# FOX attention: a pair of heads scored in one segment, forget sums by products on all rows, the meta queries in one batch

## The chip, the cores and the metric

One core of a Trainium2 chip. The metric is the device time of one launch in microseconds (us), the median of several runs. Five engines work beside each other: TensorE (PE; its weight loads are PEld), VectorE (DVE), ScalarE (ACT), GpSimd (POOL) and SyncE (SP, which issues the weight DMAs). Data lie in SBUF, products arrive in PSUM, which has 8 banks of 512 float32 columns on 128 partitions.

## What is computed

A decoder over 272 tokens: 16 meta tokens and 256 real ones, 1024 features. Four layers (FOX, GLA, GDN, FOX mixers, each with a SwiGLU), then two further layers of another kind. The change concerns the FOX mixer, which stands in layers 0 and 3. After an RMS norm and the projection to q, k, v, gate and forget logits (16 heads of 64):

```python
log_f = jax.nn.log_sigmoid((f + b_f).astype(jnp.float32))
c = jnp.cumsum(log_f, axis=1).transpose(0, 2, 1)
s = jnp.einsum('bqhd,bkhd->bhqk', q, k)          # q, k normalised per head
s = jnp.where(kpos[None, :] <= qpos[:, None], s + cq[..., :, None] - ck[..., None, :], -jnp.inf)
o = jnp.einsum('bhqk,bkhd->bqhd', jax.nn.softmax(s, axis=-1), v)
out = (o * jax.nn.sigmoid(gate)) @ w_out
```

The query's own sum cq is the same along a row and drops out of the softmax; the kernel adds only the key's. Real queries come in two blocks of 128: block A sees 144 keys (the meta tokens and itself), block B all 272. The 16 meta queries see the 16 meta keys. In layer 3 the outputs of meta tokens are not needed any more, so there the meta queries are left out.

## The kernel before, in words

All projections run with features on partitions and tokens as the moving columns. float32 accuracy comes from splitting weights and activations into a high and a low part (`ring_hi`, `ring_lo` and `y_r`, `y_lo_r`, type float32r): a tile of 128 outputs is 8 x 3 products of 128x128 by up to 272 columns (line 773, called from `blocks`). Weights stream through four ring slots; ScalarE makes the high half (line 1549, `split`), VectorE the low half (line 2113), in the FOX stage each at every second tile.

The FOX projection has 32 tiles in the order q, k, v of each of the 8 head pairs (two heads of 64 features fill 128 partitions), then 8 gate tiles (`FOX_TILES`). The attention of a pair is placed between tiles: TensorE calls `middle(t)` halfway through tile t and `after(t)` behind it. Each engine runs its own program in a fixed order; semaphores connect them. For pair c:

- after tile 3c+4, part A, after 3c+5 part B, after 3c+6 part M (the meta queries, FOX 0 only). For each part: `scores`, one tile later `turn` (transposes of the probabilities), one tile later again `values`.
- `scores` (955): for both heads a float32 product of 64 rows (two instructions each), the two heads beside each other in the array, then a product of a 2-row ones matrix with the head's forget sums (high and low part, rows 0 and 1 of `f_c_r`), one for each head.
- VectorE `largest` (2258) adds the mask and takes the least value of each row in one instruction; ScalarE `exponent` (1690) takes the exponential and the row sum; VectorE `inverse` (2271); GpSimd multiplies (2932); TensorE `turn` (995) transposes into bank 4 or 5; ScalarE `take_turned` (1677) copies; TensorE `values` (1019) accumulates into bank 6, again both heads beside each other on column halves, in key blocks of 128, 128 and 16; ScalarE copies the output.
- the q and k tiles of a pair need a statistic each (`statistic`, 979: sum of squares per head, in bank 7), after the next tile. ScalarE takes logarithm and exponential (`rstd_of`, 1660), VectorE refines it by Newton steps and scales (`head_norm`, 2218; lines 2129, 2135, 2136, 2225). The k statistic may not overwrite bank 7 before the first Newton step of q has read it (`stat_taken`).
- the v tile is transposed in `middle` (988) by three transposes of 128, 128 and 16 tokens.
- the forget sums are made once by VectorE (`forget_sums`, 2228) on 16 partitions, brought by two GpSimd DMAs to two partitions (2923, 2924) and rounded there by eight copies (2927).

VectorE's order in a tile slot t: `inverse` of the slot before, `head_norm` of tile t-2, the evacuation of tile t, `largest`, then the weight split. ScalarE's: `rstd_of`, output copy, `take_turned`, `take_tokens`, the square for the statistic, the weight split, `exponent`. After the last part, gates are applied (2279), and the result is split again for the output projection `fox_out`, by GpSimd for the pairs 0 to 4 and by ScalarE and VectorE for 5 to 7.

## Time and profile before

| | |
|---|---|
| median of three runs | 2334.38 us (2331.07 to 2335.42) |
| span of the profiled execution, first to last instruction | 2328.9 us |
| the times of the runs themselves, each with what lies around the span | 2331.07, 2334.38, 2335.42 us |
| TensorE busy (matmul side) | 2246.5 us, 96% |
| VectorE busy | 1538.0 us, 66% |
| ScalarE busy | 1186.7 us, 51% |
| GpSimd busy | 603.7 us, 26% |
| mean granted clock of TensorE | 0.992 |

How to read it: the engines' times overlap, so they don't add up. A product occupies the array for less than its record lasts, since the next starts before it ends; the distance between two starts is what it costs in a full stream. float32 products are recorded as two instructions, float32r products and transposes as one. Idle time of an engine is put down to what released it. FOX 0 lies from about 10 to 181 us, FOX 1 from 1205 to 1357 us.

### The profile page before, as it was taken

The page shows a single profiled execution, that of the slowest core. Times are in us where ns is not written, and L with a number is a line of the kernel's source. Part 1 is how long each engine was busy: PE and PEld are TensorE (multiplying, and loading weights), DVE is VectorE, ACT ScalarE, POOL GpSimd, SP SyncE. Part 2 cuts the span into 40 slices and gives each one's busy share as a digit, 9 for nine tenths or more (in the row PEclk, how much of TensorE's full clock was granted, in tenths as well). Part 3 has the DMA queues.
Part 4 walks back from the last instruction along what each step waited for, and adds up shares of the span by engine and source line. Part 5 has one row for each costly group of instructions (what it writes and reads, how often), then busy time and mean ns, then how long its engine had stood idle before and what let it go on. Part 6 is the DMA issues. An engine that isn't in the chain of part 4 may idle for free.

```text
span 2328.9 us, 48307 instructions
## 1 busy us (share of the span) xinstructions
PE 2246.5 (96%) x19152; PEld 2129.8 (91%) x19152; DVE 1538.0 (66%) x2490; ACT 1186.7 (51%) x1849; POOL 603.7 (26%) x741
## 2 busy tenths in 40 slices
PE   8999999899999999899999999998999999999998
PEld 7889999899999789899998899997789998798998
DVE  6656554656555776655556566657768976767994
ACT  5555544445544643455346554544556654556653
POOL 1114211003221030122111141217135535134540
PEclk9999999999999999999999999999999999999999
DMA  5224546324546321255552345564354555343554
GB/s 211 92 92 164 179 154 192 125 87 161 172 162 192 115 74 56 73 169 175 160 174 102 109 163 181 165 202 149 109 191 164 182 168 177 107 145 127 187 171 131
DMA packets 53007, 344.03 MB, mean 148 GB/s; under 512 B 5920, under 2 KB 7136, under 8 KB 20448
## 3 DMA queue, kind: packets, MB, share of 16 engines
q1 hardware_dynamic: 52128, 336.26, 43.7%
q0 software_dynamic: 704, 5.31, 0.6%
q8 instruction: 126, 2.06, 0.4%
q14 instruction: 49, 0.40, 0.1%
HBM read 340.43 MB, written 1.05 MB: 147 GB/s over the span
## 4 chain that ended last, share of the span: by engine, by line
PE 80%; DVE 9%; ACT 5%; issue 3%; DMA 1%; POOL 1%; DVEq 0%; ACTq 0%; SPq 0%; POOLq 0%
PE ps L773 78%; ACT ring_hi L1549 3%; DVE ring_lo L2113 2%; ACT arena L1549 1%; PE ps L1001 1%; DMA ring<-in 0%; DVE newt L2135 0%; DMA ring<-out 0%; DVE newt L2129 0%; PE ps L1435 0%; ACT rstd L1549 0%; DVE hrs L2136 0%; DVE arena L2796 0%; DMA ring<-gdn_in 0%; ACT L1549 0%
## 5 line engine op out<-in xcount | busy, mean ns | idle before, releaser
L773 PE MATMUL ps<-arena_r,ring_hi 128*128 128x272 f32 (+1 forms) x6688 | 1578.7, 285 | 9.9 <-DVE arena_r L2628 5.5
L773 PEld LDWEIGHTS ps<-arena_r,ring_hi 128*128 128x128 f32 x6688 | 1155.1, 189 | 18.1 <-issue 11.2
L773 PE MATMUL ps<-y_r,ring_hi 128*128 128x272 f32 (+1 forms) x3424 | 1003.9, 293 | 15.4 <-DVE arena L2436 5.4
L2113 DVE TENSOR_TENSOR ring_lo<-ring,ring_hi 128x2048 fp32r<-128x2048 f32 (+3 forms) x373 | 739.8, 1984 | 360.4 <-ACT ring_hi L1549 360.0
L773 PE MATMUL ps<-y_r,ring_lo 128*128 128x272 f32 (+1 forms) x3424 | 973.2, 284 | 0.0
L773 PEld LDWEIGHTS ps<-y_r,ring_hi 128*128 128x128 f32 x3424 | 646.0, 189 | 39.4 <-issue 13.7
L1549 ACT ACTIVATE ring_hi<-ring 128x2048 fp32r<-128x2048 f32 (+3 forms) x373 | 611.6, 1643 | 89.9 <-DMA ring<-dn 47.8
L773 PEld LDWEIGHTS ps<-y_r,ring_lo 128*128 128x128 f32 x3424 | 648.2, 189 | 0.0
L773 PE MATMUL ps<-arena_r,ring_lo 128*128 128x256 f32 (+1 forms) x1632 | 463.8, 284 | 0.0
L773 PEld LDWEIGHTS ps<-arena_r,ring_lo 128*128 128x128 f32 x1632 | 307.5, 188 | 0.0
L1549 ACT ACTIVATE arena<-arena 128x272 f32<-128x272 f32 (+7 forms) x197 | 91.0, 464 | 381.3 <-DVE arena L2700 257.2
L3016 POOL CAST arena_r<-arena 128x272 fp32r<-128x272 f32 (+1 forms) x132 | 134.7, 1021 | 536.0 <-DVE arena L2702 419.5
L773 PE MATMUL ps<-arena 64*64 64x64 f32 (+18 forms) x2792 | 204.4, 264 | 12.3 <-ACT arena L1549 11.2
L773 PEld LDWEIGHTS ps<-arena 64*64 64x64 f32 (+9 forms) x2792 | 144.2, 142 | 55.5 <-issue 25.9
L3024 POOL TENSOR_SCALAR arena<-x,par 128x256 f32<-128x256 f32 (+1 forms) x91 | 88.4, 971 | 305.6 <-ACT y_r L1549 304.7
L1549 ACT ACTIVATE sq<-x 128x256 f32<-128x256 f32 (+1 forms) x120 | 50.3, 419 | 187.3 <-DVE x L2164 186.5
L1549 ACT ACTIVATE arena<-ps 128x256 f32<-128x256 f32 (+7 forms) x291 | 91.7, 363 | 75.0 <-PE ps L773 32.2
L3017 POOL TENSOR_TENSOR arena_r<-arena,arena_r 128x272 fp32r<-128x272 f32 (+1 forms) x132 | 102.4, 776 | 10.6
L2741 DVE SCALAR_TENSOR_TENSOR arena<-arena,par 128x256 f32<-128x256 f32 x176 | 99.5, 623 | 0.0
L1549 ACT ACTIVATE arena<-arena,par 128x256 f32<-128x256 f32 (+1 forms) x112 | 62.0, 582 | 67.1 <-DVE arena L2677 47.7
L1549 ACT ACTIVATE arena<-arena,neg_max 128x144 f32<-128x144 f32 (+3 forms) x104 | 47.7, 459 | 83.4 <-DVE neg_max L2267 50.3
L2932 POOL TENSOR_SCALAR arena<-arena,row_inv 128x144 f32<-128x144 f32 (+2 forms) x72 | 33.4, 469 | 212.4 <-DVE row_inv L2277 212.2
(244 smaller groups left out, 1689.7 us busy)
## 6 DMA issues: line engine op xcount, KB each, us to landing
ring<-gu SPq DMA_DIRECT2D x88, 1024.0 KB, 5.1
ring<-dn SPq DMA_DIRECT2D x64, 704.0 KB, 4.1
ring<-up SPq DMA_DIRECT2D x44, 1024.0 KB, 5.2
ring<-fox_in SPq DMA_DIRECT2D x31, 1024.0 KB, 5.2
ring<-sdn SPq DMA_DIRECT2D x32, 704.0 KB, 4.1
ring<-gdn_in SPq DMA_DIRECT2D x16, 1024.0 KB, 5.2
ring<-in SPq DMA_DIRECT2D x16, 1024.0 KB, 5.2
ring<-gla_in SPq DMA_DIRECT2D x12, 1024.0 KB, 5.1
```

What stands on the lines that cost most here:

```text
L773: return nc.tensor.matmul(dst, w, mv, start=start, stop=stop)
L1001: last = nc.tensor.transpose(ps[0:w, 4 + u % 2, q * P:q * P + un["qn"]], un["p"][0:un["qn"], a:a + w], ident[0:un["qn"], 0:un["qn"]])
L1549: return nc.scalar.activation(dst, src, f, **kw)
L2113: V.tensor_tensor(ring_lo[:, slot, cols], ring[:, slot, cols], ring_hi[:, slot, cols].bitcast(F32), ALU.subtract).then_inc(lo_ready, 2 if ...
L2741: V.scalar_tensor_tensor(out=u_cc[:, q, :], in0=u_gp[:, q, 1 + tap:1 + tap + SEQ], scalar=par[:, bass.ds(i * 24 + (w0 + 12 * b + 3 * q + 1 ...
L2932: G.tensor_scalar(p, p, row_inv[0:un["qn"], u % 4:u % 4 + 1], 1.0, ALU.mult, ALU.mult).then_inc(p_ready, 1)
L3016: step(G.tensor_copy(hi_r[:, c, :], lo[:, c, :]))
L3017: G.tensor_tensor(lo_r[:, c, :], lo[:, c, :], hi_r[:, c, :].bitcast(F32), ALU.subtract).then_inc(h_split, 1)
L3024: step(G.tensor_scalar(lo[:, c, :], src[:, c, :], pcol(gain, c), 1.0, ALU.mult, ALU.mult))
```

## The change

- The four parts A0, A1, B0, B1 of a pair become one unit: after tile 3c+4 TensorE computes, for both heads, 144 and then 272 columns of scores side by side in one bank a head (416 columns, banks 2 and 3), and VectorE and ScalarE handle four blocks in a row (`least`, `exponents`, `inverses`).
- The forget sums stay where VectorE makes them: `f_sums_r` holds the high parts on partitions 0 to 15, the low parts on 32 to 47, zero elsewhere, with the 144 keys and the 272 keys side by side. A 128x128 weight of zeros with ones in the head's two rows (`f_pick_r`, 16 of them, made by GpSimd) picks a head's: one product of 128 rows and 416 columns for a head. DMAs and copies go.
- The 16 meta keys of the two heads are put block-diagonal: `f_px` has the probabilities of head 0 in columns 0 to 15, those of head 1 in 16 to 31, zero elsewhere, and `f_vsrc` the meta tokens' values likewise, each head's features only in its own columns. All blocks turned are 128x128 (eight a pair, in `middle` of tile 3c+6, four to a bank, copied by ScalarE as 512 columns). `values` comes after tile 3c+7, ahead of the next pair's scores: one product for the meta keys of both heads, then the other key blocks on column halves, the key block that both query blocks share with 256 columns at once.
- The meta queries of all eight pairs (FOX 0) are one batch at the last pair: narrow scores into bank 5, one product for their sums, three small VectorE steps, one exponential, three more, two transposes, a widened block-diagonal copy, one product of 512 columns, two copies out. The gate and the split of their outputs for pairs 0 to 6 are three VectorE instructions after the last tile (`meta_gated`), and the first product of `fox_out0` waits for them.
- Tables: three small constants more (80 columns of the constants' load).
- ScalarE's sigmoid for the gates may start two tiles earlier.

The diff, cut to its core; the bodies that it replaces stand above:

```diff
-FOX_PARTS = {"A0": (META, META + P, 0), "A1": (META, META + P, 1), "B0": (META + P, T, 0), "B1": (META + P, T, 1), "M": (0, META, 0)}
+FOX_KEYS = [META + P, T]
+FOX_SPAN = [slice(0, META + P), slice(META + P, META + P + T)]
+FOX_QUERIES = [slice(META, META + P), slice(META + P, T)]
+FOX_LAST = 3 * (KC - 1) + 4
+META_SUMS, META_SCORED, META_LEAST, META_EXP, META_P, META_TURNED, META_SPREAD, META_SUMMED, META_TAKEN, META_SPLIT = 1, 2, 3, 4, 5, 6, 8, 9, 10, 11
...
+def fox_scored(t):
+    return (t - 4) // 3 if t % 3 == 1 and 4 <= t <= FOX_LAST else None
+def fox_turned(t):
+def fox_weighed(t):
+    return (t - 7) // 3 if t % 3 == 1 and 7 <= t <= FOX_LAST + 3 else None
...
             def fox(name, nb, tpb, kc):
                 j = int(name[-1])
-                units = fox_units(j)
-
                 first_tile = n.tile
...
+                later = META + P
+                def scores(c):
+                    pe.wait_ge(head_ready, n.head + 2 * c + 2)
+                    if c == 0:
+                        pe.wait_ge(pick_ready, j + 1)
+                        pe.wait_ge(c_ready, j + 1)
                     else:
...
+                        pe.wait_ge(max_ready, n.unit + 4 * c)
+                    for part, (keys, span, queries) in enumerate(zip(FOX_KEYS, FOX_SPAN, FOX_QUERIES)):
+                        for m in range(2):
+                            r = slice(m * FD, (m + 1) * FD)
+                            mm(ps[:, 2 + m, span], f_q[r, c, queries], f_k[r, c, 0:keys], part == 0, False)
+                    if j == 0 and c == KC - 1:
+                        meta_scores()
+                    for m in range(2):
+                        mm(ps[:, 2 + m, 0:later + T], f_pick_r[:, 2 * c + m, :], f_sums_r[:, :], False, True).then_inc(s_ready, 2)
+                def meta_scores():
+                    pe.wait_ge(ptok_ready, n.unit + 4 * (KC - 1))
+                    pe.wait_ge(meta_chain, META_SUMS)
+                    for c in range(KC):
+                        for m in range(2):
+                            r = slice(m * FD, (m + 1) * FD)
+                            mm(ps[m * 32:m * 32 + 32, 5, c * META:(c + 1) * META], f_q[r, c, 0:32], f_k[r, c, 0:META], c == 0, False)
+                    mm(ps[0:64, 5, 0:P], f_parity_r[:, :], f_msum_r.rearrange("p c k -> p (c k)"), False, True).then_inc(meta_chain, 1)
...
+                def turn(c):
+                    pe.wait_ge(p_ready, n.unit + 4 * c + 4)
+                    pe.wait_ge(metas_scaled, 2 * (KC * j + c + 1))
+                    if c:
+                        pe.wait_ge(ptok_ready, n.unit + 4 * c)
                     for m in range(2):
...
+                        blocks_ = [f_pa[:, m, META:later], f_pb[:, m, META:later], f_pb[:, m, later:T], f_px[:, m, :]]
+                        if m and c == KC - 1 and j == 0:
+                            pe.wait_ge(meta_chain, META_LEAST)
+                        for q, a in enumerate(blocks_):
+                            last = nc.tensor.transpose(ps[:, 4 + m, q * P:(q + 1) * P], a, ident)
+                        last.then_inc(pt_ready, 2)
+                def meta_turn():
+                    pe.wait_ge(meta_chain, META_P)
+                    pe.wait_ge(max_ready, n.unit + 4 * KC)
+                    nc.tensor.transpose(ps[:, 2, 0:64], f_pm[0:64, :, :].rearrange("p c k -> p (c k)"), ident[0:64, 0:64])
+                    nc.tensor.transpose(ps[:, 3, 0:P], f_vmeta[:, :], ident).then_inc(meta_chain, 1)
+                def values(c):
+                    pe.wait_ge(ptok_ready, n.unit + 4 * c + 4)
+                    pe.wait_ge(vtok_ready, n.vtok + c + 1)
+                    if c:
+                        pe.wait_ge(o_taken, j * KC + c)
+                    mm(ps[:, 6, META:T], f_vtok[:, c % 2, 2, :], f_pt[:, :, 3 * P:4 * P], True, False)
+                    for m in range(2):
+                        r = slice(m * FD, (m + 1) * FD)
+                        mm(ps[r, 6, META:T], f_vtok[:, c % 2, 0, r], f_pt[:, m, 0:2 * P], False, False)
+                    for m in range(2):
+                        r = slice(m * FD, (m + 1) * FD)
+                        last = mm(ps[r, 6, later:T], f_vtok[:, c % 2, 1, r], f_pt[:, m, 2 * P:3 * P], False, True)
+                    last.then_inc(pv_ready, 4)
+                def meta_outputs():
+                    pe.wait_ge(meta_chain, META_SPREAD)
+                    mm(ps[:, 3, :], f_mv[:, :], f_mspread.rearrange("p c q -> p (c q)")).then_inc(meta_chain, 1)
                 def middle(t):
+                    if fox_turned(t) is not None:
+                        turn(fox_turned(t))
+                        if j == 0 and fox_turned(t) == KC - 1:
+                            meta_turn()
                 def after(t):
                     if t == 1 and j == 0:
                         pe.wait_ge(consts_loaded, 16)
                     if t == 0:
                         narrow(ps[0:FH, 6, 0:T], j * P, FH, 1 + 3 * j, FH).then_inc(narrow_ready, 1)
...
+                        meta_outputs()
+                    if fox_weighed(t) is not None:
+                        values(fox_weighed(t))
+                    if fox_scored(t) is not None:
+                        scores(fox_scored(t))
                     if t:
                         part, c = FOX_TILES[t - 1]
                         if part in "qk":
                             statistic(part, c)
-                    for u in in_slot(units, t - 1):
...
                 def ready(k):
+                    if meta and k == 0:
+                        pe.wait_ge(meta_chain, META_SPLIT)
                     if k >= late:
                         pe.wait_ge(late_split, n.late + k - late + 1)
                     else:
...
+                def take_turned(c):
+                    if c:
+                        act.wait_ge(pv_ready, n.unit + 4 * c)
+                    for m in range(2):
+                        act.wait_ge(pt_ready, n.unit + 4 * c + 2 * m + 2)
+                        fn(f_pt[:, m, :], ps[:, 4 + m, :], ACT.Copy).then_inc(ptok_ready, 2)
+                def exponents(c):
+                    for u in range(4):
+                        act.wait_ge(max_ready, n.unit + 4 * c + u + 1)
+                        fn(fox_p(u), fox_p(u), ACT.Exp, scale=-1.0, bias=neg_max[:, u:u + 1], accum_out=row_sum[:, u:u + 1]).then_inc(exp_ready, 1)
...
+                    keys = slice(META + P, META + P + T)
+                    step(V.tensor_copy(f_sums_r[0:FH, keys], f_rows[0:FH, 4, :]))
+                    step(V.tensor_tensor(f_sums_r[32:32 + FH, keys], f_rows[0:FH, 4, :], f_sums_r[0:FH, keys].bitcast(F32), ALU.subtract))
+                    V.tensor_copy(f_sums_r[0:48, 0:META + P], f_sums_r[0:48, META + P:2 * (META + P)].bitcast(F32)).then_inc(c_ready, 1)
                     n.logit += 1
...
+                def least(c):
+                    if c:
+                        v.wait_ge(pt_ready, n.unit + 4 * c)
+                    elif j == 0:
                         v.wait_ge(consts_loaded, 16)
...
+                def inverses(c):
+                    if c:
+                        v.wait_ge(metas_scaled, 2 * (KC * j + c))
+                    for part in range(2):
+                        v.wait_ge(exp_ready, n.unit + 4 * c + 2 * part + 2)
+                        V.reciprocal(row_inv[:, 2 * part:2 * part + 2], row_sum[:, 2 * part:2 * part + 2]).then_inc(inv_ready, 1)
...
+                def meta_gated():
+                    v.wait_ge(meta_chain, META_TAKEN)
+                    v.wait_ge(gate_ready, n.gate + KC - 1)
+                    o, hi = f_o[:, 0:KC - 1, 0:META], f_hi_r[:, 0:KC - 1, 0:META]
+                    step(V.tensor_tensor(o, o, f_gate[:, 0:KC - 1, 0:META], ALU.mult))
+                    step(V.tensor_copy(hi, o))
+                    V.tensor_tensor(f_o_r[:, 0:KC - 1, 0:META], o, hi.bitcast(F32), ALU.subtract).then_inc(meta_chain, 1)
...
+                G.memset(f_sums_r[:, :].bitcast(F32), 0.0).then_inc(sums_clear, 1)
+                step(G.memset(f_vsrc[:, :], 0.0))
+                step(G.memset(f_px[:, :, :], 0.0))
+                if j == 0:
+                    pool.wait_ge(consts_loaded, 16)
+                    G.tensor_copy(f_parity_r[:, :], const("fox_parity"))
+                G.tensor_tensor(f_pick_r[:, :, :], over(ident[:, 0:FH], P), over(ident[:, 32:32 + FH], P), ALU.add).then_inc(pick_ready, 1)
+                if j == 0:
+                    pool.wait_ge(c_ready, 1)
+                    pool.wait_ge(sums_clear, 1)
+                    G.tensor_tensor(f_msum_r[:, :, :], each(f_sums_r[:, META + P:META + P + META].bitcast(F32), KC), over(const("fox_pair"), META), ALU.mult).then_inc(meta_chain, 1)
+                sides = halves.rearrange("p (s x) -> p s x", s=2)[:, :, 0]
+                def place(c):
+                    pool.wait_ge(evacuated, BANKS + tiles + 3 * c + 3)
+                    if c:
+                        pool.wait_ge(vt_ready, KC * j + c)
+                    metas = f_v[:, c % 2, 0:META]
+                    if j == 0:
+                        G.tensor_copy(f_vmeta[:, c * META:(c + 1) * META], metas)
+                    G.tensor_tensor(f_vsrc[:, 0:2 * META].rearrange("p (s k) -> p s k", s=2), each(metas, 2), over(sides, META), ALU.mult).then_inc(metas_placed, 1)
+                place(0)
                 for c in range(KC):
...
+                    for part, p in enumerate((f_pa, f_pb)):
+                        pool.wait_ge(inv_ready, n.inv + 2 * c + part + 1)
+                        for m in range(2):
+                            u = 2 * part + m
+                            G.tensor_scalar(p[:, m, META:], p[:, m, META:], row_inv[:, u:u + 1], 1.0, ALU.mult, ALU.mult).then_inc(p_ready, 1)
+                        G.tensor_tensor(f_px[:, part, 0:2 * META].rearrange("p (s k) -> p s k", s=2), p[:, :, 0:META],
+                                        over(row_inv[:, 2 * part:2 * part + 2], META), ALU.mult).then_inc(metas_scaled, 1)
+                    if c + 1 < KC:
+                        place(c + 1)
+                n.inv += 2 * KC
```

## Rows read from the trace of the kernel before

**Rows 1.** The page: busy shares and the clock granted to TensorE in 40 slices.

```profile
PE 2246.5 (96%) x19152; PEld 2129.8 (91%) x19152; DVE 1538.0 (66%) x2490; ACT 1186.7 (51%) x1849; POOL 603.7 (26%) x741
...
PEclk9999999999999999999999999999999999999999
```

**Rows 2.** Busy time by window; start:end and length, each engine's us (instructions), PEclk, DMA.

```profile
20.74:23.74 3.00, 3.00 (x26) 3.00 (x25) 2.16 (x6) 1.39 (x2) 0.00 (x0) 1.00 0.21 86
30.03:33.66 3.63, 3.63 (x18) 3.52 (x17) 3.56 (x6) 1.33 (x3) 1.90 (x3) 0.53 0.04 10
38.22:180.98 142.76, 142.07 (x1138) 118.75 (x1138) 86.40 (x225) 81.43 (x234) 24.87 (x52) 1.00 0.30 100
82.36:99.18 16.82, 16.82 (x135) 13.82 (x134) 11.17 (x28) 10.67 (x30) 2.20 (x5) 1.00 0.18 64
1223.03:1356.80 133.77, 132.31 (x1034) 111.52 (x1034) 84.47 (x201) 78.14 (x214) 26.07 (x46) 1.00 0.32 107
1281.75:1297.33 15.58, 15.58 (x122) 13.08 (x121) 8.50 (x24) 8.47 (x26) 2.02 (x4) 1.00 0.42 136
```

**Rows 3.** TensorE's waits from 1205 to 1357 us: total us, times, longest.

```profile
PE ps L773 <- DVE newt L2129: 1.2, 2, 1.0
```

**Rows 4.** TensorE's timeline of a pair: start, us from start to last end, instructions.

```profile
70.97 0.52 PE L773 MATMUL ps<-arena 64*128 64x144 f32 x4
71.41 0.44 PE L773 MATMUL ps<-arena_r 2*128 2x144 f32 x2
71.78 0.73 PE L773 MATMUL ps<-sq,con 128*128 128x272 f32 x2
...
72.59 1.02 PE L773 MATMUL ps<-arena 128*64 128x128 f32 x12
73.54 0.39 PE L773 MATMUL ps<-y_r,ring_hi 128*128 128x272 f32 x1
...
76.74 0.73 PE L773 MATMUL ps<-arena 64*128 64x272 f32 x4
77.40 0.52 PE L773 MATMUL ps<-arena_r 2*128 2x272 f32 x2
77.84 0.73 PE L773 MATMUL ps<-sq,con 128*128 128x272 f32 x2
78.41 0.60 PE L1001 MATMUL ps<-con,arena 128*128 128x128 f32 x4
78.94 0.29 PE L773 MATMUL ps<-arena 16*64 16x16 f32 x4
```

**Rows 5.** VectorE's timeline of a pair: minima, weight split, Newton step.

```profile
88.70 0.31 DVE L2267 CUSTOM_DVE_ANT_0 arena<-ps,con 128x144 f32<-128x144 f32 x1 [0.37 <-PE ps L773]
...
94.76 0.44 DVE L2267 CUSTOM_DVE_ANT_0 arena<-ps,con 128x272 f32<-128x272 f32 x1 [0.66 <-PE ps L773]
...
95.13 0.44 DVE L2267 CUSTOM_DVE_ANT_0 arena<-ps,con 128x272 f32<-128x272 f32 x1
...
95.49 2.29 DVE L2113 TENSOR_TENSOR ring_lo<-ring,ring_hi 128x2048 fp32r<-128x2048 f32 x1
...
97.83 0.42 DVE L2129 SCALAR_TENSOR_TENSOR newt<-ps,hrs 128x272 f32<-128x272 f32 x1
```

**Rows 6.** ScalarE's timeline of a pair: exponentials, then the statistic's logarithm.

```profile
89.05 0.41 ACT L1549 ACTIVATE arena<-arena,neg_max 128x144 f32<-128x144 f32 x1 [0.26 <-DVE neg_max L2267]
...
95.25 0.52 ACT L1549 ACTIVATE arena<-arena,neg_max 128x272 f32<-128x272 f32 x1 [2.54 <-DVE neg_max L2267]
...
95.77 0.51 ACT L1549 ACTIVATE arena<-arena,neg_max 128x272 f32<-128x272 f32 x1
...
96.28 0.47 ACT L1549 ACTIVATE hrs<-ps,con 128x272 f32<-128x272 f32 x1
```

**Rows 7.** GpSimd's timeline: two probabilities times the inverses of their sums.

```profile
97.95 1.15 POOL L2932 TENSOR_SCALAR arena<-arena,row_inv 128x272 f32<-128x272 f32 x2 [7.31 <-DVE row_inv L2277]
```

**Rows 8.** TensorE's timeline at the entry of FOX 0, its wait in brackets.

```profile
29.70 0.82 PE L773 MATMUL ps<-sq,con 128*128 128x272 f32 x2 [2.33 <-DVE newt L2129]
```

281 lines of the change are left out of this document (105 added, 176 removed).

## The prediction

> **What bounds the kernel now.** I read the page's shares first, then two stretches as windows, TensorE's waits, and one pair of heads as a timeline on each engine. TensorE's matmul side is busy 96% of the span and its granted clock is full almost everywhere [rows 1]: the end is set by how much TensorE has to issue. The change touches the two FOX stages. From the first pair's scores to the last projection tile they take 142.76 us (FOX 0) and 133.77 us (FOX 1), with VectorE busy 60 to 63% of that [rows 2]. TensorE waits little there: 1.2 us on VectorE from 1205 to 1357 us, most of it at the stage's entry [rows 3]. So what is taken off TensorE's own stream shortens the kernel, until another engine is late.
>
> Durations overlap in the pipeline, so I price by the distance between starts [rows 4]. A projection tile of 24 products is 3.00 us when nothing interrupts it (first window of [rows 2]). A steady pair (three tiles, 9.0 us) takes 16.82 us in FOX 0 and 15.58 us in FOX 1 [rows 2]; 7.8 us of the former are attention.
>
> **Prices from [rows 4].** Scores of both heads: 0.45 us at 144 keys (70.97 to 71.41), 0.66 us at 272. The 128 further columns in 2 instructions a head cost 0.21 to 0.22 us, so one column in one instruction is 0.84 ns (two passes), both heads beside each other. Then 144 columns need 0.24 us and 272 need 0.46; the other 0.20 us is what changing the shape in which the array is used (64x128 after 128x128, and away again) costs. The forget products on 2 rows: 0.37 and 0.44 us for two single-pass products that should stream 0.12 and 0.23, again 0.2 of change. A statistic is 0.57 us (77.84 to 78.41) with one such change, 0.46 without. Four transposes plus the change behind them are 0.53 us: 0.11 each, whether 16 or 128 columns wide. The 12 value instructions are 0.95 us (72.59 to 73.54).
>
> **The change part by part, one pair.**
> - Scores: one segment of 144 and 272 keys with one change of shape: 0.24 + 0.46 + 0.20 = 0.90 us (before 0.45 + 0.66, and 0.33 for the pair's meta cells).
> - Forget sums: two products on 128 rows over 416 columns, single pass: 416 x 0.42 ns = 0.18 each, and 0.10 for going back to the full array: 0.47 us (before 0.37 + 0.44). No row of before has 416 columns: below it is bounded by 0.35 (no change cost), above by 0.35 + 0.20 + 0.10.
> - Statistics: both now follow full-array work, 2 x 0.46 = 0.92 us (before some 0.66 + 0.57).
> - Values: a full-array product of 256 columns (0.43), then column halves 256 (0.43) and 128 columns (0.22), changes 0.25: 1.33 us. Streamed columns hardly fall (640 against 656); three groups become one. Between 1.2 and 1.5.
> - Transposes: 8 in one go 0.87 us and 3 for the values 0.33; none of them changes the shape. The 16-column ones already cost as much as whole ones.
>
> Sum 4.82 us, so a pair is 9.0 + 4.8 = 13.8 us of TensorE in FOX 0, 13.65 in FOX 1, where a query tile streams 256 columns (3.00 - 24 x 16 x 0.42 ns = 2.84 us).
>
> The stretches: FOX 0 = 27 tiles 81.1 + 8 x 1.37 scores and sums 11.0 + values 10.8 + 14 statistics 6.4 + 7 x 0.33 + 8 x 0.87 = 118.6, and the batch for the meta queries: 32 narrow score instructions (some 0.03 each with changes: 1.2), the parity product and two transposes 0.3, one product over 512 columns 0.86: 2.3. That is 120.9 us. FOX 1 = 13 tiles at 3.00, 14 at 2.84, and 37.5: 116.3 us.
>
> **What becomes late.** This is the part that can undo it. TensorE's next fixed points after a pair's scores are the key statistic of the next pair (it shares a bank with the query statistic, so it waits until VectorE's first Newton step has read that), and the pair's turn, half a tile later. Let X be the end of tile 3c+4. Values now go ahead of scores: the first head's scores stand at X + 1.33 + 0.90 + 0.29 + 0.2 latency = X + 2.7 (before X + 1). VectorE's queue is then: four minima (0.3, 0.3, 0.37, 0.36 [rows 5]) to X + 4.0; in every other pair the weight split, 2.29 us, to X + 6.2; the reciprocals, which wait for all exponentials; the Newton step, 0.42. ScalarE: four exponentials 0.41, 0.41, 0.52, 0.51 from X + 3.05, to X + 4.9, then the statistic's logarithm and exponential 0.93, to X + 5.85 [rows 6]. TensorE is back after 3.16 us of this group and a tile of 3.0, at X + 6.16.
>  - pairs with the split behind the minima (even c): Newton step to X + 6.7, with TensorE's answer 0.15 later: 0.7 us late, and 0.1 since the idle engine shows its weight load. GpSimd gets the inverses at X + 6.3 and needs four multiplications (1.15 us for a pair of 272 [rows 7], some 0.8 for the short ones) and two small ones of about 0.3: it is done at X + 8.9, where TensorE wants to turn: 0.1 to 0.2 more. Together 0.95.
>  - odd c: Newton step to X + 6.3: 0.4 us.
>  The last pair has no next statistic: 4 x 0.95 + 3 x 0.4 = 5.0 us a stage. Nothing later in the pair is late: turned probabilities are in SBUF near X + 10.5, the values want them at X + 13.8; VectorE has some 10 us of work in 14. The cost is between 0 (everything hides) and 1.6 a pair (both splits in the way and GpSimd slowed by VectorE as in its slower rows).
>  - entry: the sums get a third copy on VectorE ahead of the Newton step for which TensorE already waited 2.33 us [rows 8]: 0.3 us a stage. The gathering DMAs and eight casts leave GpSimd; the 128x2048 weight of ones and zeros comes in, some 4 us beside tiles 0 and 1, hidden; without that cover it would delay scores 0, due 20 us later.
>  - exit of FOX 0: the output projection's first product now waits until VectorE, behind tile 31, has multiplied and split the meta columns of seven pairs: 0.55 + 3 x 0.3 = 1.5 us in which TensorE has nothing. A wait of about 0.4 us some tiles later for VectorE goes in exchange: 1.1 us net. Queued behind these three on VectorE is the last pair's gate and split, needed only at k = 7, 2.6 us after the start.
>
> The Trainium skill, TensorE: Matmul & The Clock Gate, Part 3 (The mechanism), says that weight loads overlap with running matmuls "only when row_grp differs". By that rule each product moved to all 128 rows would show its weight load. The trace disagrees: the tile's 24 products, all on 128 rows, each with its own weights, are 0.125 us apart, which leaves no such time [rows 2].
>
> **Sum.** FOX 0: 142.76 - 120.9 - 5.0 = 16.9 saved; FOX 1: 133.77 - 116.3 - 5.0 = 12.5; entries -0.6, exit -1.1: 27.7 us. On the profiled execution: 2328.9 - 27.7 = 2301.2 us of span. The median of the runs, 2334.38, lies 5.5 us over that span (start and end outside it, and scatter of 4 us between runs); carried along: 2306.7, say 2306 us.
>
> **Rivals.**
> - A, nothing is late: VectorE and ScalarE answer in time. For: they idle a third of the stage. Against: the queue order above. 10 us more are saved: 2296.
> - B, waits twice what I count or more: 1.3 us a pair on top, 14 pairs, +18: 2324. For: the minima and exponentials of a pair now come in one burst ahead of the statistic, and GpSimd's two multiplications of 1.15 us ran beside VectorE [rows 7], with which its work may collide oftener. Against: each term of the chain is a duration measured beside such work.
> - C, slower: the waits cost clock. At the FOX 0 entry a wait of 2.33 us was followed by 3.6 us at a granted clock of 0.53 (the 1.2 GHz level) [rows 2, 8], in which 18 instructions took the time of 29: 1.4 us lost. If the key statistic waits as long in each pair: 14 x (2.3 - 0.7 + 1.4) = 42 us, so 2348. It decides from a chain 1.6 us longer than the one above; against it, the longest wait of 1.0 us at the entry of FOX 1 [rows 3], my 0.7 being less than that.
> - D, the change does not bring the saving named: the shape changes cost as much in one long segment as in three, say because the halves contend for their banks when eight run in a row. Then only meta cells and a few transposes go: 0.8 us a pair less saved, +13 and more: 2320; its chance is small, for the value instructions run at 0.11 us a pair of halves inside their group.
> - E, weight loads show on each of the three products a pair that move to 128 rows: at some 0.1 each (half of a 0.20 change): 3 x 0.1 x 16 = 5 us: 2311. Against: the 0.125 us of the tile's products [rows 2]. The page cited above would have it so.
>
> **How the numbers follow.** My forecast 0.64, A 0.11, B 0.13, C 0.06, D 0.04, E 0.02. Range: A's 2296 less a microsecond, up to most of B: 2295 to 2322. A measurement of this kernel tells 0.2%, 4.7 us, from no change. Faster by more: all but C and the far ends of B and D, 0.88; within 0.2%: 0.04; slower: 0.08.
>
> **What would show it.** Steady pair near 14.6 us (FOX 0) and 14.4 (FOX 1), against 16.8 and 15.6; turns as eight equal steps of 0.11 us; the scores segment 0.9 us, two sums products 0.18 apart; TensorE's largest wait inside the stages on the Newton step, more in even pairs; one idle stretch of 1 to 2 us ahead of FOX 0's output projection; full clock in both stretches; all other stages the same to 1 us. I am wrong if the pairs stay over 16 us, if the clock falls inside the stages, or if the gain appears outside these two stretches.

## The result and the profile after

The changed kernel takes 2318.66 us (median of 4 runs, 2315.65 to 2321.79), against 2333.84 for the kernel before beside it. The medians lie 15.2 us apart; the ratio of the runs, 0.9942 [0.9928, 0.9956] (the bracket is its 95% interval), is 13.5 us, between 10.3 and 16.8. The forecast was 2306, 27.7 us less: the sign is right, the size 12.5 us too large. The profiled execution ran 2317.68 us with a span of 2315.9.

From the page of the changed kernel: busy shares, and the granted clock in 40 slices.

```profile
PE 2222.5 (96%) x18861; PEld 2126.9 (92%) x18861; DVE 1532.6 (66%) x2446; ACT 1177.9 (51%) x1720; POOL 623.7 (27%) x777
...
PEclk9999999999999999999999999999999999999999
```

TensorE is still the bound, with 24.0 us less of busy time than in [rows 1]. The busy time of windows (columns as in [rows 2]): FOX 0 from the first scores to the end of tile 31, two steady pairs of FOX 0, two of FOX 1.

```profile
40.17:167.47 127.30, 123.07 (x959) 110.99 (x958) 82.85 (x192) 75.22 (x161) 36.30 (x72) 1.00 0.33 112
54.14:83.54 29.40, 28.35 (x217) 25.45 (x216) 19.20 (x46) 17.79 (x39) 7.78 (x16) 1.00 0.32 108
...
1246.28:1275.41 29.13, 28.00 (x216) 25.11 (x215) 19.10 (x45) 17.79 (x39) 7.46 (x14) 1.00 0.33 109
```

FOX 0's stretch is 127.3 us where 142.76 stood [rows 2]: 15.5 saved, 16.9 forecast. A steady pair is 29.40 / 2 = 14.7 us (forecast 14.6) and 14.57 in FOX 1 (forecast 14.4). One pair on TensorE:

```profile
68.45 2.30 PE L780 MATMUL ps<-arena 128*128 128x256 f32 x18
70.68 0.64 PE L780 MATMUL ps<-arena_r 128*128 128x416 f32 x2
71.16 0.62 PE L780 MATMUL ps<-sq,con 128*128 128x272 f32 x2
71.41 0.49 PE L780 MATMUL ps<-y_r,ring_hi 128*128 128x272 f32 x1
...
75.37 0.47 PE L780 MATMUL ps<-sq,con 128*128 128x272 f32 x1 [0.59 <-DVE newt L2150]
```

Values and scores together take 2.23 us (68.45 to 70.68) for 1.33 + 0.90 forecast, the two sums products 0.48 for 0.47. The key statistic at 75.37 waits for the Newton step, as the prediction said of the even pairs: the weight split of 2.29 us stands in front of it (started at 72.46). TensorE's waits in FOX 0's stretch, nearly all for that step (total, times, longest):

```profile
PE ps L780 <- DVE newt L2150: 3.6, 7, 1.1
PE ps L1013 <- issue: 0.7, 3, 0.2
```

FOX 1's stretch has 3.5 us for that step and 0.9 us for GpSimd's multiplications ahead of three turns (line 1013). The clock stays full in both stretches.

So the priced part came true. What did not lies ahead of the pairs, at the two entries, and in stages that the change does not touch. TensorE's wait at the entry of FOX 1 (window from the norm's sum of squares to the first scores), and what the clock did there:

```profile
PE ps L780 <- DVE newt L2150: 3.3, 1, 3.3
```

```profile
1209.64:1213.05 3.41, 2.87 (x11) 2.67 (x12) 3.31 (x7) 1.92 (x3) 1.10 (x1) 0.50 0.00 0
```

The longest wait there was 1.0 us before [rows 3] and the clock was full; now it is 3.3 us (1206.92 to 1210.18), and from 1209.64, within this wait, the clock is at its 1.2 GHz level for 3.41 us. The stretch is 21.46 us instead of 17.88. FOX 0's entry, where TensorE had waited 2.33 us [rows 8], has a wait of 3.5.

The cause stands in the timelines of GpSimd and VectorE there. First FOX 0 (start, us, instruction):

```profile
22.71 3.60 POOL L2986 TENSOR_TENSOR arena_r<-con 128x2048 fp32r<-128x2048 f32 x1
```

```profile
23.01 0.42 DVE L2235 TENSOR_TENSOR arena<-ps,rstd 16x272 f32<-16x272 f32 x1
23.46 3.00 DVE L2236 TENSOR_SCALAR arena<-arena,par 16x272 f32<-16x272 f32 x1
26.39 2.27 DVE L2134 TENSOR_TENSOR ring_lo<-ring,ring_hi 128x2048 fp32r<-128x2048 f32 x1
```

In the kernel before the same instruction took 0.35 us, and the Newton step's second instruction at FOX 1's entry 0.44:

```profile
22.69 0.35 DVE L2216 TENSOR_SCALAR arena<-arena,par 16x272 f32<-16x272 f32 x1
...
1207.26 0.44 DVE L2135 SCALAR_TENSOR_TENSOR newt<-newt,rstd 128x272 f32<-128x272 f32 x1
```

The TENSOR_SCALAR now ends at 26.46, just behind the end of GpSimd's table of ones and zeros (22.71 + 3.60 = 26.31); the one ahead of it, with PSUM as one source, keeps its 0.42. Then FOX 1, in the order GpSimd, VectorE:

```profile
1197.50 3.61 POOL L2986 TENSOR_TENSOR arena_r<-con 128x2048 fp32r<-128x2048 f32 x1
```

```profile
1198.47 0.44 DVE L2150 SCALAR_TENSOR_TENSOR newt<-ps,rstd 128x272 f32<-128x272 f32 x1 [1.81 <-ACT rstd L1558]
1198.95 2.46 DVE L2156 SCALAR_TENSOR_TENSOR newt<-newt,rstd 128x272 f32<-128x272 f32 x1
1201.44 0.44 DVE L2157 SCALAR_TENSOR_TENSOR rstd<-newt,rstd 128x272 f32<-128x272 f32 x1
```

Two sources in SBUF: 2.46 us while the table runs, 0.44 behind it. The table was not idle work beside others; it stopped the engine that the whole stage's entry waits for. The Trainium skill, SBUF — State Buffer, section "SBUF: two separate sides", calls the port pair that GpSimd and VectorE share "an **exclusive lock**, not a bandwidth split" for VectorE instructions in a mode that uses both ports or with two SBUF inputs; the trace agrees, 3.00 us for 0.35 and 2.46 for 0.44, with PSUM readers beside it unharmed.

FOX 1's entry is 3.58 us longer. The Newton step for which TensorE waits starts 12.77 us behind the norm's sum of squares (1209.60) where it was 10.50 us: 2.0 of these 2.3 us are the held instruction, 0.23 the third copy of the sums (line 2258). The other 1.3 us come with the fall of the clock.

Where the difference in time lies, by the trace (span 13.0 us shorter): to the end of FOX 0's mixer 12.5 saved, FOX 1 with its entry 7.2 saved, the untouched stages 6.7 lost. Of these, 4.4 lie in the GLA stage (409 to 559 us in the kernel before, first row; the changed kernel second), where the clock was lower, and 2.5 behind FOX 1.

```profile
409.39:558.95 149.56, 142.10 (x1093) 135.81 (x1092) 93.27 (x135) 70.94 (x81) 29.10 (x29) 0.99 0.35 117
```

```profile
396.89:550.85 153.96, 145.03 (x1093) 138.15 (x1092) 92.29 (x135) 70.91 (x81) 28.79 (x29) 0.97 0.34 113
```

FOX 0's first scores come at 40.17 instead of 38.22. Some 0.8 us of that are the start of the profiled execution and not the kernel's: in the same 1.80 us the kernel before got 13 products through, the changed one 8, since TensorE's clock rose 1.9 us earlier in that execution. The column PEclk doesn't show this, for the trace has no record of the clock ahead of its first rise, and the column then prints 1.00. The distance between starts does: 0.213 us until 10.32 in the changed kernel, 0.111 us from 9.71 on in the kernel before. First row before, second after:

```profile
9.70:11.50 1.80, 1.80 (x13) 1.46 (x12) 1.52 (x3) 1.37 (x4) 0.00 (x0) 1.00 0.98 410
```

```profile
9.70:11.50 1.80, 1.80 (x8) 1.57 (x8) 1.45 (x3) 0.54 (x3) 0.00 (x0) 1.00 0.96 401
```

The profile of the kernel before is also not the usual one at this place. The three other profiles without the change and without the table (columns_before, columns_64 and one_warm_product below) have the same wait of 2.3 us, but no fall of the clock behind it, and their first scores come at 37.98 to 38.06 although their clock rose as late as 12.2 to 12.7 us. In all nine profiles with the change (waits of 3.1 to 4.3 us), and in table_alone (2.8 us), the clock falls there. The same window in the kernel before, in columns_before and in the changed kernel, with the granted clock as the third number from the right:

```profile
20.00:38.00 18.00, 15.67 (x110) 15.07 (x108) 14.22 (x25) 8.42 (x14) 6.76 (x9) 0.91 0.37 124
```

```profile
20.00:38.00 18.00, 15.66 (x123) 14.68 (x121) 15.56 (x25) 7.86 (x13) 5.44 (x7) 1.00 0.39 127
```

```profile
20.00:38.00 18.00, 14.48 (x101) 13.73 (x99) 17.23 (x26) 7.79 (x12) 6.63 (x5) 0.91 0.26 94
```

### The profile page after: what moved, and what is told of

The parts are those of the page before. It is cut to its first block, busy times and chain, and to the rows that moved or that the text cites. A ratio compares the mean times of both kernels' runs of the same rounds, so it can differ in the third digit from the quotient of the medians.

```text
span 2315.9 us, 47394 instructions
## 1 busy us (share of the span) xinstructions
PE 2222.5 (96%) x18861; PEld 2126.9 (92%) x18861; DVE 1532.6 (66%) x2446; ACT 1177.9 (51%) x1720; POOL 623.7 (27%) x777
## 4 chain that ended last, share of the span: by engine, by line
PE 80%; DVE 8%; ACT 6%; issue 4%; DMA 2%; POOL 1%; DVEq 0%; SPq 0%; ACTq 0%; POOLq 0%
PE ps L780 77%; ACT ring_hi L1558 3%; DVE ring_lo L2134 2%; ACT arena L1558 1%; PE ps L1013 1%; DVE newt L2150 0%; DMA ring<-in 0%; DMA ring<-out 0%; ACT hrs L1558 0%; DVE newt L2156 0%; DVE arena L2290 0%; PE ps L1444 0%; ACT rstd L1558 0%; DVE arena L2855 0%; ACT y_r L1558 0%
## 5 line engine op out<-in xcount | busy, mean ns | idle before, releaser
L780 PE MATMUL ps<-arena_r,ring_hi 128*128 128x272 f32 (+1 forms) x6688 | 1583.8, 286 | 10.8 <-DVE arena_r L2687 5.5
L780 PE MATMUL ps<-arena 64*64 64x64 f32 (+17 forms) x2602 | 189.8, 266 | 11.3 <-ACT arena L1558 10.2
L780 PEld LDWEIGHTS ps<-arena 64*64 64x64 f32 (+8 forms) x2602 | 138.5, 144 | 46.1 <-issue 19.0
L1558 ACT ACTIVATE arena<-ps 128x512 f32<-128x512 f32 (+5 forms) x174 | 81.9, 491 | 84.0 <-PE ps L780 31.4
L3097 POOL TENSOR_TENSOR arena_r<-arena,arena_r 128x272 fp32r<-128x272 f32 (+1 forms) x132 | 102.2, 774 | 10.6
L2185 DVE TENSOR_TENSOR x<-ps,x 128x256 f32<-128x256 f32 (+1 forms) x112 | 48.0, 429 | 64.1 <-PE ps L780 64.0
L3088 POOL CAST arena_r<-arena 128x256 fp32r<-128x256 f32 (+1 forms) x40 | 20.8, 519 | 253.2 <-DVE arena L2859 131.2
```

The lines of the kernel that those rows point to most:

```text
L780: return nc.tensor.matmul(dst, w, mv, start=start, stop=stop)
L1558: return nc.scalar.activation(dst, src, f, **kw)
L2185: V.tensor_tensor(dst[:, c, :], take(c, width), dst[:, c, :], ALU.add).then_inc(evacuated, 1)
L3088: step(G.tensor_copy(hi_r[:, c, :], lo[:, c, :]))
L3097: G.tensor_tensor(lo_r[:, c, :], lo[:, c, :], hi_r[:, c, :].bitcast(F32), ALU.subtract).then_inc(h_split, 1)
```

## The experiments

The first four were timed beside the kernel before at 2331.93 us (9 runs).

**again**: the changed kernel, unaltered.

> The changed kernel once more, nothing edited. In its first profile the GLA stage (from the norm sum behind the first down projection to the one behind GLA's output projection) took 153.96 us against 149.55 before, with one stretch at half clock more. Theory 'luck of the clock': in this profile the stage is anywhere between 149.5 and 154 us, in step with the stretches at half clock in it; the two FOX stretches stay within 0.5 us of 127.3 and their entries stay as long. Rival 'caused by the change': the GLA stage is again 154 us, and in every profile of a kernel with this change. Time: 2318.7 plus or minus 3 us, 15 us under the kernel before.

2319.84 us (2317.05 to 2324.49), ratio 0.9951 [0.9937, 0.9964]. Again 21.7 us of entry at FOX 1 with a fall of the clock. The GLA stage took 150.90 us where the first profile had 153.96. So the rival "caused by the change, again 154" is out, but luck alone isn't shown either: over all profiles below the stage takes 150.9 to 151.1 us in three of the nine with the change and 154.0 to 154.1 in six, and 149.6 to 152.6 in the five without it, 2.0 us less on average. The stages behind FOX 1 took 6.4 us more than in the kernel before in this profile, against 2.5 in the first.

**scores_first**: a pair's scores ahead of the values of the pair before.

```diff
-                    if fox_weighed(t) is not None:
-                        values(fox_weighed(t))
                     if fox_scored(t) is not None:
                         scores(fox_scored(t))
+                    if fox_weighed(t) is not None:
+                        values(fox_weighed(t))
```

> One edit to the changed kernel: behind tile 3c+4 TensorE issues the new pair's scores before the values of the pair before. Theory 'late chain': the key statistic waits since minima, exponentials and the query statistic's Newton step start 1.33 us late behind the values; with scores first, steady pairs of FOX 0 fall from 14.31 and 15.09 us to about 13.8 and 14.0, those of FOX 1 likewise, 7 pairs a stage: 10 to 13 us less than the changed kernel, about 2306 us. Rival 'engines are full': VectorE's and ScalarE's work per pair sets the pace and not the order; then pairs stay within 0.2 us of 14.7 on average and the time is the same. Number of changes of the array's shape is the same in both orders.

2313.11 us, ratio 0.9921 [0.9907, 0.9934]: 6.7 less than again. Two steady pairs, and TensorE's waits over the stage:

```profile
54.33:68.39 14.06, 14.06 (x108) 12.74 (x107) 10.19 (x23) 7.94 (x19) 4.46 (x8) 1.00 0.36 117
68.39:82.45 14.06, 14.06 (x109) 12.75 (x108) 9.12 (x23) 9.74 (x20) 3.04 (x8) 1.00 0.31 110
```

```profile
PE ps L780 <- DVE newt L2150: 1.1, 1, 1.1
```

A pair falls from 14.7 to 14.06, and each FOX stage by 3.8 us; the wait stays only at the first pair. The expectation was 10 to 13 us, since it had the pairs at 13.8 and 14.0. So the waits of the prediction were real and near the size given (forecast 5.0 a stage), and they came from the place it named: values first put the minima 1.3 us later. What is left above 13.8 is 0.3 us a pair.

**table_alone**: the kernel before, with GpSimd's 128x2048 table instruction put in its place in the stage; its output is not used.

```diff
                 G.tensor_copy(f_ones_r[0:2, :], ones[0:2, :])
+                if j == 0:
+                    pool.wait_ge(consts_loaded, 16)
+                step(G.tensor_tensor(view_r(4352, FH, P)[:, :, :], over(ident[:, 0:FH], P), over(ident[:, 32:32 + FH], P), ALU.add))
```

> The kernel before with one thing added: at each FOX entry GpSimd makes the 128x2048 table in one instruction of 3.6 us, at the place where the changed kernel does; nobody uses it. Theory 'held back': a VectorE instruction that reads only SBUF and starts beside it ends only with it (0.35 us becomes 3.0 in FOX 0, 0.44 becomes 2.5 in FOX 1 in the changed kernel), and the entry's chain through VectorE gets longer: FOX 0's first scores 1 to 1.6 us later after the stage's begin, FOX 1's 2 to 3.5 us (with a fall of the clock) later; 3 to 5 us more in all, about 2338 us. Rival 'third copy': the loss at the entry comes from the sums' third copy and the semaphores around it; then this kernel is within 1 us of the kernel before and its VectorE instructions keep their 0.35 and 0.44 us.

2340.7 us, ratio 1.0041 [1.0028, 1.0055]: 8.8 slower, more than any theory gave it. The entry of FOX 1 is 20.69 us (17.88 before), with a fall of the clock at 1220.6 that the kernel before has not. The rows of GpSimd and VectorE at FOX 1:

```profile
1207.55 3.60 POOL L2924 TENSOR_TENSOR arena_r<-con 128x2048 fp32r<-128x2048 f32 x1
```

```profile
1209.24 0.44 DVE L2129 SCALAR_TENSOR_TENSOR newt<-ps,rstd 128x272 f32<-128x272 f32 x1 [1.81 <-ACT rstd L1549]
1209.72 1.73 DVE L2135 SCALAR_TENSOR_TENSOR newt<-newt,rstd 128x272 f32<-128x272 f32 x1
```

1209.72 + 1.73 = 1211.45, GpSimd's end 1211.15. At FOX 0 the same TENSOR_SCALAR takes 2.58 us (from 23.89) and ends 0.15 us behind the table. The mechanism is shown on the old kernel, and rival 'third copy' is out as its cause. The profiled execution, 2334.94 us, is the shortest of the five: its span is 4.2 us above that of the kernel before, and the entries (1.7 at FOX 0, where a late rise without a fall of the clock gave 38.0 in other profiles, and 2.8 at FOX 1) account for all of it. What the median has beyond that, 4.6 us, is not placed.

**table_pieces**: the table as 16 instructions of 128x128.

```diff
-                G.tensor_tensor(f_pick_r[:, :, :], over(ident[:, 0:FH], P), over(ident[:, 32:32 + FH], P), ALU.add).then_inc(pick_ready, 1)
+                for h in range(FH):
+                    last = G.tensor_tensor(f_pick_r[:, h:h + 1, :], over(ident[:, h:h + 1], P), over(ident[:, 32 + h:33 + h], P), ALU.add)
+                last.then_inc(pick_ready, 1)
```

> One edit to the changed kernel: the table is made in 16 instructions of 128x128 in place of one of 128x2048. Theory 'held back': a VectorE instruction then waits for at most one piece (about 0.3 us), so the two entries (from the norm sum to the first scores) lose 1 and 2 to 3 us: 3 to 4 us less than the changed kernel, 2315 us. Rival 'bandwidth': GpSimd and VectorE share a rate, so the pieces slow VectorE as much in sum: within 1 us of the changed kernel. Rival 'third copy': no change either.

2315.77 us, ratio 0.9927 [0.9914, 0.9941]: 4.1 less than again, with intervals that just overlap. FOX 1's entry is 18.45 us and the clock stays full in it; the Newton step there takes 0.68 us instead of 2.46. FOX 0's entry gained nothing (first scores at 40.26, 40.46 in again), and its rows say why:

```profile
23.70 0.37 DVE L2236 TENSOR_SCALAR arena<-arena,par 16x272 f32<-16x272 f32 x1
25.70 2.57 DVE L2134 TENSOR_TENSOR ring_lo<-ring,ring_hi 128x2048 fp32r<-128x2048 f32 x1 [1.63 <-ACT ring_hi L1558]
...
28.55 0.63 DVE L2251 SCALAR_TENSOR_TENSOR arena<-arena 16x272 f32<-16x272 f32 x1
29.21 0.80 DVE L2253 TENSOR_TENSOR_SCAN arena<-arena 16x272 f32<-16x272 f32 x1
```

VectorE is free at 24.07 instead of 26.5, but it then waits for ScalarE's half of the weight split, which begins at 25.70, 0.7 us earlier than in the changed kernel. The pieces are drawn out until 31.5, and beside them VectorE's instructions get longer: the split 2.57 for 2.27, the two behind it 0.63 for 0.42 and 0.80 for 0.71, the three copies of the sums 0.2 together. These 0.8 us eat the gain up: the Newton step starts at 31.20, where it was 31.09. At FOX 0 the rival 'bandwidth' thus described what happened, at FOX 1 the theory 'held back'.

These four left the loss in untouched stages open. Behind FOX 1 their products are the same ones in the same order, yet slower: in 160 us of the last SwiGLU, where all moving operands have 256 columns and nothing waits, the kernel before starts 1361 products and the changed one 1350 (first row before, second after).

```profile
2140.00:2300.00 160.00, 159.78 (x1361) 159.59 (x1360) 138.74 (x194) 91.35 (x109) 66.84 (x44) 1.00 0.55 177
```

```profile
2130.00:2290.00 160.00, 159.86 (x1350) 159.68 (x1349) 136.76 (x189) 88.38 (x107) 66.77 (x44) 1.00 0.55 179
```

The mean distance of two products there is 117.4 and 118.4 ns; in the stages with 272 columns it is 125.4 in both. The change had added 80 columns to the constants, and behind these lie the small weights and the arena, with the low halves of the activations in it. The next four were timed beside the kernel before at 2332.46 us (23 runs).

**columns_before**: the kernel before with 80 unused constant columns.

```diff
 _const("fox_mask", P + META + T + META)
+_const("unused", 80)
```

> The kernel before, with one edit: 80 unused columns among the constants, so that everything allocated behind them (small weights, squares, the arena with the low parts of the activations) lies 80 columns further on, as in the changed kernel. Why: in all four profiles of kernels with the change, the products of 256 columns in the stages after FOX 1 (untouched code) start 118.0 to 118.5 ns apart, in both profiles without it 117.4 to 117.8; over some 6500 products that is 4 to 5 us that the change does not seem to owe to its own work. Theory (place of the data): pitch 118.0 to 118.4 ns here too, time before + 4 to 5, so 2336 to 2337 us. Rival (it is TensorE's instruction stream, whose layout in memory the change moves): pitch 117.4 to 117.8 and the time of before, 2332 within 2.

2336.06 us (11 runs), ratio 1.0016 [1.0007, 1.0024]: 3.6 us slower with nothing but addresses changed, 1.6 to 5.6 by the interval. Its window:

```profile
2140.00:2300.00 160.00, 159.86 (x1348) 159.63 (x1347) 138.11 (x196) 91.82 (x109) 67.09 (x45) 1.00 0.54 175
```

**columns_128**: the changed kernel with 48 further unused columns.

```diff
-_const("fox_pair", KC); _const("fox_row", KC); _const("fox_parity", 64)
+_const("fox_pair", KC); _const("fox_row", KC); _const("fox_parity", 64); _const("unused", 48)
```

> The changed kernel, with 48 further unused columns among the constants, so that all behind them lies 128 columns instead of 80 further on than before. Theory (the place of the data decides, and a multiple of 128 columns is as good as the old place): pitch of the products of 256 columns back to 117.4 to 117.8 ns, time 2319.8 - 4 to 5 = 2315. Rival (instruction stream): pitch stays 118.0 to 118.4 and the time at 2320 within 2.

The pitch is back, the time not clearly: 2319.35 us, 0.5 us under again, not the 4 to 5 expected. The ratio is 0.9936 [0.9924, 0.9948]; that of again, 0.9951 [0.9937, 0.9964], would make it 3.5 us, with intervals that overlap.

```profile
2130.00:2290.00 160.00, 159.77 (x1361) 159.58 (x1360) 139.38 (x195) 91.36 (x110) 66.84 (x44) 1.00 0.54 178
```

**one_warm_product**: the kernel before, one more float32 product at its start.

```diff
-START_WARM = 8
+START_WARM = 9
```

> The kernel before with nine instead of eight float32 products on constants at its start, while TensorE waits for the tokens: four instructions more stand ahead of everything in TensorE's stream. Theory (place of the data): nothing moves, pitch 117.4 to 117.8, 2332 us within 2 (the start can lose 0.2 us). Rival (instruction stream): pitch of the 256-column products may change, to anything between 117.4 and 118.5, and the time with it by up to 5 us; no change would not exclude it, since another shift is tried than the one that the change makes.

2333.02 us, ratio 1.0002 [0.9993, 1.0011]. The pitch kept to 117.4 to 117.8 in five of the seven stages behind FOX 1 and was 116.1 to 116.3 in two, never above: by itself it does not exclude the instruction stream, but the pitch moved with the columns alone in columns_before and came back in columns_128, so nothing of the pitch is left for it to explain.

**three_together**: table in pieces, scores first, and `meta_gated` ahead of the evacuation of tile 31.

```diff
+                    if j == 0 and t == 31:
+                        meta_gated()
                     evacuate(t, part, c)
...
-                if j == 0:
-                    meta_gated()
                 gated(KC - 1)
```

> The changed kernel with three edits: the table as 16 instructions of 128x128, a pair's scores ahead of the values of the pair before, and meta_gated ahead of the evacuation of tile 31. By the runs so far the first is worth 4.1 us (2319.84 to 2315.77), the second 6.7 (to 2313.11). meta_gated takes 0.84 us behind the evacuation while TensorE has nothing; ahead of it, it should run in the last tile's shadow: 0.8 us. Theory (the three waits are apart from each other and add up): 2319.8 - 4.1 - 6.7 - 0.8 = 2308.2, within 2. Rival (the clock or the next wait takes part of it): 2311 to 2314.

2305.56 us (2304.78 to 2307.03), ratio 0.9882 [0.9868, 0.9897]. The three add up, and a little more: 14.3 us under again where 11.6 were expected. Behind tile 31 VectorE's order is now

```profile
162.42 0.27 DVE L2323 TENSOR_TENSOR arena<-arena 128x112 f32<-128x112 f32 x1
162.73 0.22 DVE L2324 CAST arena_r<-arena 128x112 fp32r<-128x112 f32 x1
162.98 0.27 DVE L2325 TENSOR_TENSOR arena_r<-arena,arena_r 128x112 fp32r<-128x112 f32 x1
163.23 0.44 DVE L2277 TENSOR_TENSOR arena<-ps,rstd 128x272 f32<-128x272 f32 x1
```

where in the changed kernel the evacuation came first (167.67) and the split ended at 168.86, with TensorE waiting 1.33 us. Here it waits 0.17 us.

The last four were timed beside the kernel before at 2329.06 us (17 runs).

**again_2**: the changed kernel once more.

> The changed kernel unaltered, as the companion of the other three in the same call. All theories: 2319.8 within 2; pitch of the 256-column products behind FOX 1 118.0 to 118.5 ns.

2319.35 us, ratio 0.9952 [0.9937, 0.9968].

**columns_128_2**: as columns_128.

> The changed kernel with 48 further unused constant columns, a second time: the pitch went back to 117.4 to 117.7 ns in its first profile, which is 4 to 5 us, but the time stayed at 2319.35, with a mean clock of 0.987 to 0.991 in its six runs against 0.989 to 0.991 in those of the changed kernel. Theory (the saving is real and the first six runs had more time at half clock by scatter): 2315 to 2317 beside 2319.8 for the changed kernel in this call. Rival (in this kernel the shorter pitch is paid back at half clock): 2319 to 2320 again, mean clock 0.988.

2316.72 us, ratio 0.9939 [0.9924, 0.9955]: 2.6 less than again_2, as the first theory had it, with a mean clock of 0.987 to 0.990 against 0.988 to 0.991. The intervals overlap, so the saving is likely and not shown.

**three_and_columns**: three_together with the 48 columns.

> The three edits of three_together (table as 16 instructions, scores ahead of values, meta_gated early) and the 48 further columns. three_together ran at 2305.56. Theory (place of the data is worth 3.6 to 4.7 us here as well): 2301 to 2302. Rival (paid back at half clock): 2305 to 2306, mean clock 0.988.

2302.84 us (2301.45 to 2307.2), the lowest median of all, but its ratio 0.9886 [0.9868, 0.9904] is that of three_together on another chip. The pitch is 116.1 to 117.9 in all stages behind FOX 1; the theory of 3.6 to 4.7 us isn't borne out, and what the whole kernel has of it is not separated from the scatter.

**columns_64**: the kernel before with 64 unused columns instead of 80.

```diff
 _const("fox_mask", P + META + T + META)
+_const("unused", 64)
```

> The kernel before with 64 unused constant columns instead of 80: all behind them lies 256 bytes further on in each partition. With 80 (320 bytes) the pitch of the 256-column products rose from 117.5 to 118.2 ns and the time by 3.6 us. Theory A (a place at a multiple of 64 columns is as good as the old one): pitch 117.4 to 117.8, time 2332 to 2333. Theory B (only multiples of 128 columns keep the old place): pitch 118 or more, 2335 to 2337.

2328.68 us (12 runs), ratio 0.9999 [0.9989, 1.0008]. Its window:

```profile
2140.00:2300.00 160.00, 159.78 (x1371) 159.56 (x1371) 140.21 (x199) 93.38 (x112) 66.79 (x44) 1.00 0.56 181
```

64 columns (256 bytes a partition) do no harm, 80 (320 bytes) do.

## Why the prediction was right, and where it was wrong

- **What bounds**: right. The end followed TensorE's stream; the two stretches gave 15.5 and 11.1 us of the 16.9 and 12.5 forecast.
- **Prices of the pair**: right to a few hundredths (scores 0.90, sums 0.48, values 1.32 by the starts, turns 0.79 to 0.82 for 0.87). One slip: 8 values at 1.33 are 10.6 us, not the 10.8 in the sum. Rival D is out: one long segment cost what the sum gave it. Rival E is out: the second sums product, with weights of its own on 128 rows, is followed after 0.19 us, for 0.18 streamed. (The first is followed after 0.29, so the two are not 0.18 apart as expected; the change of shape shows there.)
- **What becomes late, in the pairs**: right in place (Newton step, more in even pairs) and nearly in size: 14.7 and 14.57 for 14.6 and 14.4, 2.9 us less saved over both stretches. scores_first took 3.8 a stage of the 5.0 away. Rival B is out: the waits are 4.3 and 4.4 us in the two stages, not the double of 5.0. Rival A's pairs without waits, 13.8, are nearly reached with the other order (14.06).
- **Entry: the step that failed.** "The 128x2048 weight of ones and zeros comes in, some 4 us beside tiles 0 and 1, hidden" asked only when the table is needed, 20 us later, and not what it does to its neighbour while it runs. Forecast for entries 0.6 us, of which the third copy's 0.23 us a stage (line 2258) came true. Measured in the trace: 3.6 at FOX 1 and 1.95 at FOX 0. At FOX 1, table_pieces took 3.0 to 3.3 of them away, with the fall of the clock that the longer wait brought. At FOX 0, 0.8 is the start's late clock; the remaining 1.2 are the held instruction (0.9) and the third copy (0.2), and table_pieces returned none of it, for its pieces slowed the instructions behind. This compares with a profile whose clock also fell there; against the three that had no fall, the first scores of the nine profiles with the change come 1.5 to 3.2 us later, and part of that is the clock. Rival C had the right mechanism, a longer wait that costs clock, in the wrong place: not at each pair but at the entries.
- **Exit of FOX 0**: right. TensorE waited 1.33 us, forecast 1.5; net 1.0, forecast 1.1.
- **"All other stages the same to 1 us"**: wrong, and by the trace the largest part of the miss: 6.7 us. The prediction named the three constants in the change and gave them no price. They move the arena by 320 bytes, and the 256-column products behind FOX 1 stand 0.4 to 1.0 ns further apart: 6800 of them at 0.7 on average, at most 4.8 us, of which this trace shows 2.5 and columns_before 3.6 (1.6 to 5.6). The other 4.4 us lie in the GLA stage, in step with the clock, 3.1 of them gone in again.

The account of the miss, by the trace (27.7 forecast, 13.0 measured, 14.7 short): pairs 2.9, FOX 1's entry 3.3, FOX 0's 1.6, exits 0.2, GLA 4.4, behind FOX 1 2.5, other stages 0.2 gained. The medians miss by 12.5, so a single profile carries some 2 us that the others don't. Shown by an experiment are the pairs' part, that of FOX 1's entry, and the effect of the columns in the kernel before; in the changed kernel taking that back gave 0.5, 2.6 and, in three_and_columns, nothing clear of the scatter. That 2318.66 lies inside the forecast range is luck: the range reached up there for rival B, which did not happen.

Not settled is the clock. The mean clock of the changed kernel's runs is 0.988 to 0.991 where the kernel before has 0.991 to 0.993 in most; 0.002 of 2320 us are 4.6 us, which is an estimate of what it costs where TensorE is never idle. The fall at FOX 1's entry is explained by the table, the one at FOX 0's comes with the change in nine profiles of nine and without it in one of four. A fall early in the GLA stage is in all profiles of kernels with the change and also in those of columns_before, one_warm_product and columns_64, so the change is not needed for it; but it lasts twice as long (6.8 us) only in six of the nine with the change.

## What to carry to other kernels

A long GpSimd instruction that reads SBUF was not free here even where nobody waited for its result: look at which VectorE instructions without a PSUM source fall beside it, and at who waits for them. Short pieces let them through, but slow what runs beside them, so they help where little stands beside (FOX 1, 3 us) and not where much does (FOX 0, nothing). When an untouched stage changes, count its instructions in equal windows and look at what moved in memory, constants too. Between two groups with the same work, the one whose answer is needed sooner goes first.

## What the hardware showed that was not expected

- The distance of float32r products with 256 moving columns depends on where the data behind the constants lie: 117.4 to 117.8 ns at the old place (116.1 to 116.3 in two stages of one_warm_product), 117.9 to 118.5 with all moved by 80 columns (up to 119.0 in one short stage), and 117.4 to 117.9, in some stages 116.1 to 116.3, with 64 or 128. Products of 272 columns kept 125.4. Why is open; which of the moved tensors does it was not tried.
- Four VectorE instructions held by GpSimd ended 0.15 to 0.3 us behind it, whatever their own length: 3.00 and 2.58 for 0.35 us, 2.46 and 1.73 for 0.44.
- The first rise of TensorE's clock came between 9.7 and 13.0 us in profiles of kernels with the same start. The stage's products on the forget weights began at 17.73 us with the earliest rise and at 19.20 with the latest, so a single profile's early landmarks carry up to 1.5 us of that.
